# Attention in a two-layer hybrid decoder: one exponential for two heads in pairs of banks, and row scores in parts of 512 keys

## The reference, cut to what matters

```python
def _causal_attention(q, k, v):
    T = q.shape[1]
    scale = 1.0 / float(np.sqrt(q.shape[-1]))
    bounds = [(0, N_META)] + [(s, min(s + ATTN_BLOCK, T)) for s in range(N_META, T, ATTN_BLOCK)]
    outs = []
    for s, e in bounds:
        sc = jnp.einsum('bqhd,bkhd->bhqk', q[:, s:e], k[:, :e],
                        preferred_element_type=jnp.float32) * scale
        causal = jnp.arange(e)[None, :] <= jnp.arange(s, e)[:, None]
        sc = jnp.where(causal[None, None], sc, -jnp.inf)
        probs = jax.nn.softmax(sc, axis=-1).astype(v.dtype)
        outs.append(jnp.einsum('bhqk,bkhd->bqhd', probs, v[:, :e]))
    return jnp.concatenate(outs, axis=1)
```

## Time and profile before

| | us |
|---|---|
| time, median of 3 runs | 3749.19 (3748.92 to 3755.58) |
| the profiled execution, its own time | 3753.3 |
| its span, first to last instruction | 3751.4 |
| TensorE busy | 3591.0 (96%) |
| DVE busy | 2383.3 (64%) |
| ACT busy | 1308.7 (35%) |
| POOL busy | 1414.1 (38%) |

### The profile page before, as it was taken

One profiled execution on the slowest core, in us unless ns is written; L12 is line 12 of the kernel. 1 busy time (PEld: TensorE's weight loads), 2 busy tenths in 40 slices (PEclk: granted clock), 3 DMA queues, 4 the chain that ended last, 5 costly groups with the idle time before them and its releaser, 6 DMA issues. The chain is left out here.

```text
span 3751.4 us, 69222 instructions
## 1 busy us (share of the span) xinstructions
PE 3591.0 (96%) x29059; PEld 3284.4 (88%) x29059; DVE 2383.3 (64%) x2811; ACT 1308.7 (35%) x1898; POOL 1414.1 (38%) x819
## 2 busy tenths in 40 slices
PE   7999999999999999999999999999999999999998
PEld 6667988988798999999985689898869989999998
DVE  2265447655469877776833743585655698777687
ACT  5243124312213444453433430441231144444435
POOL 4064940000252565544412659100004535555341
PEclk9999999999999999999999999999999999999999
DMA  5430766522332222263234238564324122222732
GB/s 118 115 82 29 246 215 184 159 68 69 129 91 74 74 74 83 83 246 129 85 72 131 60 96 266 165 196 118 82 70 142 51 80 87 79 80 74 263 124 84
DMA packets 475704, 438.10 MB, mean 117 GB/s; under 512 B 105807, under 2 KB 400939, under 8 KB 475419
## 3 DMA queue, kind: packets, MB, share of 16 engines
q1 hardware_dynamic: 455164, 382.22, 33.9%
q10 hardware_dynamic: 20255, 51.78, 3.8%
HBM read 296.88 MB, written 137.05 MB: 116 GB/s over the span
## 5 line engine op out<-in xcount | busy, mean ns | idle before, releaser
L280 POOL TENSOR_TENSOR w_hi<-w_raw,consts 128x1024 fp32r<-128x1024 f32 (+1 forms) x78 | 127.9, 1640 | 1193.7 <-DMA w_raw<-in_w_proj_rwkv 826.3
L234 PE MATMUL psum<-h_hi,w_hi 128*128 128x348 f32 x1632 | 355.6, 327 | 9.5 <-ACT lat_sq L815 3.6
L234 PE MATMUL psum<-h_lo,w_hi 128*128 128x348 f32 x1632 | 349.3, 322 | 0.0
L234 PE MATMUL psum<-h_hi,w_lo 128*128 128x348 f32 x1632 | 348.0, 322 | 0.0
L234 PEld LDWEIGHTS psum<-h_hi,w_hi 128*128 128x128 f32 x1632 | 276.0, 189 | 17.8 <-ACT lat_sq L815 3.8
L234 PEld LDWEIGHTS psum<-h_lo,w_hi 128*128 128x128 f32 x1632 | 277.7, 189 | 0.0
L234 PEld LDWEIGHTS psum<-h_hi,w_lo 128*128 128x128 f32 x1632 | 275.3, 188 | 0.0
L3184 PE MATMUL psum<-t_hi,piece_hi_w 128*128 128x260 f32 x1280 | 258.4, 283 | 5.1 <-issue 2.6
L3139 POOL TENSOR_TENSOR piece_lo_w<-sum,piece_hi_w 128x512 fp32r<-128x512 f32 x120 | 209.2, 1744 | 140.7 <-ACT piece_hi_w L3452 137.7
L3184 PE MATMUL psum<-t_lo,piece_hi_w 128*128 128x260 f32 x1280 | 258.1, 283 | 0.0
L3184 PE MATMUL psum<-t_hi,piece_lo_w 128*128 128x260 f32 x1280 | 257.2, 282 | 0.0
(11 more groups left out here) (598 smaller groups left out, 9519.9 us busy)
## 6 DMA issues: line engine op xcount, KB each, us to landing
w_raw<-in_w_in SPq DMA_DIRECT2D x68, 512.0 KB, 9.6
wsum<-in_w_down SPq DMA_DIRECT2D x88, 256.0 KB
wsum_scratch<-wsum SPq DMA_DIRECT2D x22, 1024.0 KB
raw_g<-in_w_up SPq DMA_DIRECT2D x40, 512.0 KB, 3.8
raw_v<-in_w_up SPq DMA_DIRECT2D x40, 512.0 KB, 3.9
gate_scratch<-gst ACTq DMA_DIRECT2D x32, 522.0 KB, 3.0
gbuf<-gate_scratch SPq DMA_DIRECT2D x32, 522.0 KB, 3.5
prep_scratch<-prep ACTq DMA_DIRECT2D x8, 2080.0 KB, 8.3
```

The lines of the kernel that those rows point to most:

```text
L234: last = nc.tensor.matmul(bank[:, n, :], w(k), x(k)[:, nrange(n)], start=(k == 0 and q == 0), stop=(k == kt - 1 and q == 2))
L280: nc.gpsimd.tensor_tensor(w_hi[s][:, 0:width], w_raw[s][:, 0:width], consts[:, 4:5].broadcast_to([P, width]), ALU.mult).then_inc(hi_done.s ...
```

## The change

The ring of slots in banks 4 to 7 now has two slots of two banks, 4-5 and 6-7. The scores of both heads go side by side into one slot, and ACT takes one exponential over both. M and RS take a slot each and use its first bank. The outputs move to banks 2 and 3. Row scores have two slots of one bank, 0 and 1, and all rows longer than 512 keys are taken in parts of at most 512 keys; the two or three partial maxima are combined by a `tensor_reduce` where a `tensor_tensor` was used for the last block. A pair has 30 row pieces instead of 20, and their places in the steps are new. TensorE waits once more at the end, before the product for the next phase, whose banks 0 to 2 now include one of the output banks.

```diff
-        nm_last = [after(f"nm_last{e}", [P, 2]) for e in range(2)]
+        nm_last = [after(f"nm_last{i}", [P, 3]) for i in range(4)]
...
         def row_parts(b):
             n = b * BLK + rows_of(b)
-            return ((0, n),) if n <= 1024 else ((0, 1024), (1024, n))
+            return tuple((at, min(at + 512, n)) for at in range(0, n, 512))
...
-            if g == 0 and s < 3:
-                return [(0, *r) for r in rows_in(1)[2 * s:2 * s + 2]]
-            if s < 8:
-                first, more = ((2 * (s - 3), 2) if s < 6 else (s, 1)) if g == 0 else ((s // 2) + s - 1, 1 + s % 2) if 0 < s < 6 else (0, 0)
-                return [(g, *r) for r in own[first:first + more]]
+            table, source = (FIRST_AT, rows_in(1) + own) if g == 0 else (OWN_AT, own)
+            if s in table:
+                first, more = table[s]
+                return [(g, *r) for r in source[first:first + more]]
...
-        AHEAD_AT = {11: (0, 3), 12: (3, 2), 14: (5, 3), 15: (8, 2), 16: (10, 2)}
+        AHEAD_AT = {11: (0, 3), 12: (3, 3), 14: (6, 3), 15: (9, 4), 16: (13, 3)}
+        OWN_AT = {n: (2 * n, 2) for n in range(7)}
+        FIRST_AT = {0: (0, 4), 1: (4, 3), 2: (7, 3), **{3 + n: (10 + 3 * n, 3) for n in range(4)}, 7: (22, 2)}
...
             def row_view(m, lo, hi, rows):
-                return psum[0:rows, 2 * (m % 2):2 * (m % 2) + 2, :].rearrange("p b n -> p (b n)")[:, lo:hi]
+                return psum[0:rows, m % 2, lo:hi]
...
-                ring += [("S", n, e) for e in range(2)] + [("M", *x) for x in shifts_at(n)] + [("RS", *x) for x in sums_at(n)]
+                ring += [("S", n)] + [("M", *x) for x in shifts_at(n)] + [("RS", *x) for x in sums_at(n)]
...
             def ring_bank(x):
-                return 4 + ring_no[x] % 2
+                return 4 + 2 * (ring_no[x] % 2)
...
             def y_bank(n):
-                return 6 + group_no(n) % 2
+                return 2 + group_no(n) % 2
...
                 def scores(n, e):
-                    x, p = ("S", n, e), g % 2
-                    if ring_taken(x):
+                    x, p = ("S", n), g % 2
+                    if e == 0 and ring_taken(x):
                         pe.wait_ge(acts.sem, acts.of(0, ring_taken(x)))
...
-                    out = psum[0:kb, ring_bank(x), 0:w]
+                    bank = ring_bank(x) + e
+                    out = psum[0:kb, bank, 0:w]
...
                 pe.wait_ge(next_lo, 8)
+                pe.wait_ge(dves.sem, dves.of(0, f"y{RT - 1}_{NG - 2}"))
...
-                def exponent(n, e):
+                def exponent(n):
                     q0, w, off, kb = cut(n)
-                    act.wait_ge(pes.sem, pes.of(0, f"S{n}_{e}"))
+                    act.wait_ge(pes.sem, pes.of(0, f"S{n}_1"))
...
-                    acts.did(nc.scalar.activation(pt[n % NPT][0:kb, e, 0:w], psum[0:kb, ring_bank(("S", n, e)), 0:w], ACT.Exp), f"exp{n}_{e}")
+                    bank = ring_bank(("S", n))
+                    acts.did(nc.scalar.activation(pt[n % NPT][0:kb, :, 0:w], psum[0:kb, bank:bank + 2, 0:w], ACT.Exp), f"exp{n}")
...
                 def maximum(g, b, e, part):
...
-                    if part:
+                    if part and part == len(names) - 1:
                         for name in names:
                             dve.wait_ge(dves.sem, dves.of(0, name))
-                        dves.did(nc.vector.tensor_tensor(col, nm_last[e][0:rows, 0:1], nm_last[e][0:rows, 1:2], ALU.min), f"mx{g}_{b}_{e}")
+                        dves.did(nc.vector.tensor_reduce(col, last[0:rows, 0:len(names)], AX.X, ALU.min), f"mx{g}_{b}_{e}")
```

More of the change, by code:

```diff
@@ L994, in max_names @@
         def max_names(g, b, e):
-            return [f"mx{g}_{b}_{e}"] if len(row_parts(b)) == 1 else [f"mx{g}_{b}_{e}a", f"mx{g}_{b}_{e}b"]
+            return [f"mx{g}_{b}_{e}"] if len(row_parts(b)) == 1 else [f"mx{g}_{b}_{e}" + x for x in "abc"[:len(row_parts(b))]]
         pe_n, act_n, dve_n, pool_n = [], [], [], []
@@ L1004, in layer @@
                 pe_n += [f"S{n}_{e}" for e in range(2)]
-                act_n += [f"exp{n}_{e}" for e in range(2)]
+                act_n.append(f"exp{n}")
             pe_n += [f"R{r[0]}_{r[1]}_{r[2]}_{r[3]}" for r in rows] + [f"M{x}_{G}" for x, G in shifts] + [f"RS{x}_{G}" for x, G in sums]
@@ L1012, in layer @@
             for x, b, e, part in rows:
-                dve_n += [max_names(x, b, e)[part]] + ([f"mx{x}_{b}_{e}"] if part else [])
+                dve_n += [max_names(x, b, e)[part]] + ([f"mx{x}_{b}_{e}"] if part and part == len(row_parts(b)) - 1 else [])
             for x, G in sums:
@@ L1122, in add @@
                     acc_, now = racc[gi % 2], pt[n % NPT]
-                    for e in range(2):
-                        pool.wait_ge(acts.sem, acts.of(0, f"exp{n}_{e}"))
+                    pool.wait_ge(acts.sem, acts.of(0, f"exp{n}"))
                     if c == (0 if G == 0 else 1) and gi >= 2:
@@ L1169, in rows_of_scores @@
                     q = q_hi[g % 2][e][0:QK, b * BLK:b * BLK + rows]
-                    for at in range(lo, hi, 512):
-                        end = min(at + 512, hi)
-                        last = mm(row_view(m, at - lo, end - lo, rows), q, k_hi[g % 2][e][0:QK, at:end], start=True, stop=True)
+                    last = mm(row_view(m, 0, hi - lo, rows), q, k_hi[g % 2][e][0:QK, lo:hi], start=True, stop=True)
                     if hi == b * BLK + rows:
@@ L1210, in scores @@
                     if c in blocks_in(G):
-                        last = mm(psum[0:kb, ring_bank(x), 0:kb], ident_r[0:kb, 0:kb], mask_col[0:kb, 0:kb], start=False, stop=True, skip_group_check=True)
+                        last = mm(psum[0:kb, bank, 0:kb], ident_r[0:kb, 0:kb], mask_col[0:kb, 0:kb], start=False, stop=True, skip_group_check=True)
                     pes.did(last, f"S{n}_{e}")
@@ L1220, in outputs @@
                         pe.wait_ge(dves.sem, dves.of(0, "y{}_{}".format(*divmod(group_no(n) - 2, NG))))
-                    for e in range(2):
-                        pe.wait_ge(acts.sem, acts.of(0, f"exp{n}_{e}"))
+                    pe.wait_ge(acts.sem, acts.of(0, f"exp{n}"))
                     for e in range(2):
@@ L1287, in _ @@
                     g, s = divmod(n, PS)
-                    for e in range(2):
-                        exponent(n, e)
+                    exponent(n)
                     for x in shifts_at(n):
@@ L1311, in maximum @@
                     dve.wait_ge(pes.sem, pes.of(0, f"R{g}_{b}_{e}_{part}"))
-                    col = maxima_col(g, b, e)
+                    col, last = maxima_col(g, b, e), nm_last[2 * (b % 2) + e]
                     if (g, b) == (0, 3) and not e:
                         dve.wait_ge(pools.sem, pools.of(0, "zero1"))
-                    dst = col if len(names) == 1 else nm_last[e][0:rows, part:part + 1]
+                    dst = col if len(names) == 1 else last[0:rows, part:part + 1]
                     dves.did(nc.vector.tensor_reduce(dst, row_view(m, 0, hi - lo, rows), AX.X, ALU.max, negate=True), names[part])
-                    if part:
+                    if part and part == len(names) - 1:
                         for name in names:
                             dve.wait_ge(dves.sem, dves.of(0, name))
-                        dves.did(nc.vector.tensor_tensor(col, nm_last[e][0:rows, 0:1], nm_last[e][0:rows, 1:2], ALU.min), f"mx{g}_{b}_{e}")
+                        dves.did(nc.vector.tensor_reduce(col, last[0:rows, 0:len(names)], AX.X, ALU.min), f"mx{g}_{b}_{e}")
                 def low(g, x, e):
@@ L1338, in divide @@
                     dve.wait_ge(pes.sem, pes.of(0, f"O{g * PS + END_OF[G]}"))
-                    dves.did(nc.vector.tensor_tensor(y[:, 0:w], psum[:, 6 + gi % 2, 0:w], y[:, 0:w], ALU.mult), f"y{g}_{G}")
+                    dves.did(nc.vector.tensor_tensor(y[:, 0:w], psum[:, 2 + gi % 2, 0:w], y[:, 0:w], ALU.mult), f"y{g}_{G}")
                 for n in range(NS):
```

## The result

The changed kernel took 3792.9 us in the median of 4 runs (3783.6 to 3803.7) against 3749.1 (3748.9 to 3755.6): ratio 1.0117, 95% interval 1.0098 to 1.0135. I had forecast 3762, at most 3777. The direction was right, the size was short by 31 us.

A forecast was written before the change was run, and what follows sets the result against it. Attention was taken as bound by TensorE's in-order stream. Direct terms of +11.4 us and +1.5 for the clock gave +12.9, on 3749.2 a forecast of 3762 us; own range 3755 to 3770, whole range 3736 to 3777.

The forecast's parts named there:

- What bounds the stage: Causal attention: bound by TensorE's stream in order; an edit is worth the idle time it takes out or puts in.
- The single exponential: ACT, both heads in one: 0.82 or 0.63 us, result 0.33 us (0.23) later but hidden behind scores: 0.
- D: Rival: late exponential not hidden in steps 7 to 10, +5.5 us, 3767; chance 0.48 together with the forecast.
- The ring's slots: Two-bank slots for scores: waits on ACT fall 1.8 us per pair, 1.4 kept, 1.0 in the last pair.
- The hold-back by ACT's conversions: Next pair's first rows wait for ACT's conversion of q, so 0.7 us of gain ahead becomes 0.3.
- The row slots: Two single-bank slots: each reopens 1.23 to 1.35 us after its row began; third rows wait 0.65 us or more.
- step 12: Pairs 1 and 2: a new third row waits 1.4 us, behind the q_lo subtraction in DVE's queue.
- The sum of all direct terms: Per layer: pair 0 +4.5, pairs 1 and 2 +2.2, pair 3 -1.0, together +5.7; two layers +11.4 us.
- TensorE's clock: Attention: one more stretch at half clock after the new waits, +1.5 us; bounds -4.5 and +15.
- Rival C: Waits every 2 to 3 us bring ten more stretches at half clock, +26 us, 3776; chance 0.12.
- The combination: Partial maxima on DVE: one-input reduction needs no port shared with GpSimd, so ten per pair cost about 0.15 us each.
- The wait ahead of the next product: End of attention: waits on the next-to-last group's division, which ends some 4 us before: 0.

The follow-up runs named there:

- rows_only: Kernel before with the change's row part alone (512-key parts, two single banks, new places in steps), ring and per-head exponentials as before: 3829.9 us, ratio 1.0216.
- the short pair: Changed kernel and kernel before, each with maxima over 16 columns and exponentials scaled by 2^-12: 3750.9 us (ratio 0.9995) and 3741.3 us (0.9971).
- after_again: The changed kernel run once more with no edit: 3802.4 us, ratio 1.0137 to the kernel before.
- rows_four: rows_only with four single banks for the 512-key row parts where it had two: 3747.4 us, ratio 0.9991 to the kernel before.
- fill: rows_only with useless matmuls put ahead of each third or later row of a step, where TensorE waits: 3814.0 us, ratio 1.0167 to the kernel before.
- after: The changed kernel as first measured, against the kernel before: 3792.9 us, ratio 1.0117.
- after_tt: The changed kernel with the two-part maxima combined by tensor_tensor where it had tensor_reduce: 3813.0 us, one run.
- spread: The changed kernel with the next pair's rows spread over steps 9 to 17, at most two in a step but for pair 0: 3779.6 us, ratio 1.0072.
- four_spread: rows_four with the next pair's rows spread over steps 9 to 17, at most two in a step: 3744.9 us, ratio 0.9986 to the kernel before.

## Why the prediction was right in direction and wrong in size

- **What bounds the stage: right.** All but 2.4 us of the 30.4 us of span are in the two phases, and TensorE's idle time and clock decide.
- **The single exponential: right.** 0.811 and 0.621 us (0.82 and 0.63 forecast), 144 instead of 288; its later result (D) was not seen as a loss.
- **The ring's slots: right in its own rows, 1.4 us per pair kept being too much.** pt and q_hi fell from 13.7 to 7.8 us. By rows_only against the changed kernel its worth can't be told (4.4 us by one number, less than nothing by the other), by the short pair it is nothing; I had 10 to 11. The hold-back by ACT's conversions, which I took at 0.4 us per pair, ate more: 3.1 us in layer 1 of the changed kernel (L1300).
- **The row slots: the mechanism right, the amounts somewhat small.** A slot reopened after 1.29 us (1.23 to 1.35), the third row waited 0.70 (0.65), step 12 waited 1.42 (1.4), and the first M came 9.5 us after the first scores instead of 7.6, +1.9 (+1.8). Pair 1 at the full clock grew by 1.8 (1.1), pair 0 of layer 0 by 5.8 at nearly equal clock (4.5), and pair 3 shrank by about 2 (1.0). The waits on DVE were 4.5 us in pair 1 of layer 1 (above 2.5), but 11.2 in pair 0 of layer 0, where I had said some 6. The sum of all direct terms, +11.4 us, was measured as +10.1 less the clock and +15.5 in idle time (+9.6 and +15.8 in after_again), so it lies between the two.
- **TensorE's clock: the step that failed.** "I take one more: +1.5." It was 12.5 to 18 us in this profile and 20 to 26 in after_again. The price of one short low stretch, 1.5 us, was taken from single ones, and the bound of +15 was too narrow for after_again. I counted the stretches before (three after single waits) and added one, instead of asking what happens to a stream in which 27 waits in a layer have 19 us. The stretches didn't come singly any more: one lasted 20 us. That such waits are what lowers the clock is shown by rows_four (the waits gone, 7 us at 1.2 GHz left of 112) and by fill (the waits filled, 4 left); how much comes of a given set of waits is not: the same 37 us of idle time went with 47, 63 and 99 us at 1.2 GHz in after, after_again and after_tt. Rival C named this mechanism at 3776 with a chance of 0.12; even it was short by 17 us.
- **The combination: right** (0.155 us each). The alternative at the mean of 0.89 us was wrong for the price of tensor_tensor in these places: 0.37 in after_tt.
- **The wait ahead of the next product: 0**, as forecast; no such wait is in the rows.

What stays open: outside the attention phases, times differ between kernels by up to 12 us in code that is the same. The five profiles with the changed ring have 3395.2 to 3400.2 us there, the eight without it 3388.5 to 3395.6, a difference of 7 us in the means. So a few microseconds of the change may lie outside the phases that this account is about, and go with the ring; in the first pair of profiles it is 2.4 us. The cause is not known: it was not tried. Nor was a kernel that keeps the changed ring and has more than two row banks, which eight banks don't allow.

## What to carry to other kernels

When a buffer is cut into smaller parts, count how many instructions the producer can run ahead, not only the bytes: here the same DVE work cost 82 us more with two slots than with four. Price each new wait of a TensorE-bound stage twice, once for its length and once for the clock. Where waits of about half a microsecond recurred here, 27 of them in a phase of 197 us, the second price was as large as the first or larger (12.5 to 26 us against 10 to 16), and it differed from execution to execution. And before a ring is deepened, look at what the engine will meet next: 7 us of waits removed became 10 us of others.

## What the runs showed of the hardware

- Short waits that recur can lower TensorE's clock: 21.6 us of waits for DVE in layer 1 of the changed kernel, none over 2.1 us, went with 31.6 us at 1.2 GHz. The kernel before had 5.1 us of them there and no low stretch (in layer 0, three short ones, 10.9 us in all). Matmuls put into such waits brought 112 us at 1.2 GHz down to 4.
- Once low, the clock can stay at 1.2 GHz through 20 us in which TensorE waits little (2183 to 2203 above, 233 to 251 in spread). The same 18 steps then took 41.7 instead of 34.7 us.
- How much of it comes differs between executions of one kernel: 3784 to 3806 us over the eight runs of the changed kernel, 3739 to 3752 over the first ten of four_spread and 3733 to 3752 over twelve more. With fewer waits there can be more of it in a single profile: spread had 67 us at 1.2 GHz and 28.3 us of idle time, the changed kernel 47 and 36.9.
- A small tensor_tensor on DVE can be held until a GpSimd addition beside it ends: 1.83 us instead of 0.16. A tensor_reduce in the same places took 0.14 to 0.16 us in all of 80.
